# One matmul with 32 copies of each bias column in place of four with 128

## The reference, cut to what matters

```python
bias_h = rel_bias.astype(jnp.float32).T            # (4 heads, 32 buckets)
...
dist_own = qp[:, None] - (qblk * BLK + offs)[None, :]
s_own = (jnp.einsum('bhqd,bhkd->bhqk', qc, kown)
         + bias_h[:, t5_bucket(jnp.maximum(dist_own, 0))][None])
s_own = jnp.where(dist_own >= 0, s_own, NEG_INF)
```

## Time and profile before

| what | us |
| --- | --- |
| median of 3 runs | 1577.85 (1576.73 to 1578.09) |
| the profiled execution's own time | 1576.61 |
| its span, first to last instruction | 1574.8 |
| PE busy | 1333.2 (85%) |
| DVE busy | 423.2 (27%) |
| ACT busy | 278.7 (18%) |
| POOL busy | 180.0 (11%) |
| DMA, mean over the span | 316 GB/s |

### The profile page before, as it was taken

How to read it: one execution, slowest core, us unless ns; L and a number is a source line. 1 busy time by engine, 2 the same in 40 slices (tenths; PEclk the granted TensorE clock), 3 DMA queues, 4 the chain that set the end, 5 groups by cost and what they waited for, 6 DMA issues and landing times. The chain is left out here.

```text
span 1574.8 us, 22184 instructions
## 1 busy us (share of the span) xinstructions
PE 1333.2 (85%) x9378; PEld 719.3 (46%) x9378; DVE 423.2 (27%) x842; ACT 278.7 (18%) x544; POOL 180.0 (11%) x122
## 2 busy tenths in 40 slices
PE   9999999999999999776776767899999676676776
PEld 4855456545879564322322323655554232232332
DVE  3443343523565531120000100257321010010011
ACT  2132310323412121210000000105211111011010
POOL 0450033300000005692000000000000000000000
PEclk9999999999999999898898999999999989899789
DMA  9923442254640499999999999944799999999997
GB/s 383 346 81 140 180 160 107 80 187 161 231 160 31 165 387 405 429 427 429 429 427 429 428 427 429 387 183 165 285 406 426 427 427 427 428 427 426 429 427 323
DMA packets 44867, 498.20 MB, mean 316 GB/s; under 512 B 6656, under 2 KB 8960, under 8 KB 12544
## 3 DMA queue, kind: packets, MB, share of 16 engines
q1 hardware_dynamic: 44800, 497.22, 77.0%
HBM read 495.11 MB, written 2.10 MB: 316 GB/s over the span
## 5 line engine op out<-in xcount | busy, mean ns | idle before, releaser
L2858 PE MATMUL banks<-weight_ring,arena 128*32 128x512 f32 x1472 | 212.9, 710 | 126.1 <-DMA weight_ring<-in_moe_weights 126.0
L2776 DVE TENSOR_TENSOR arena<-arena,banks 64x512 f32<-64x512 f32 x32 | 22.1, 690 | 656.2 <-ACT arena L2713 656.2
L2858 PEld LDWEIGHTS banks<-weight_ring,arena 128*32 128x32 f32 x1472 | 45.2, 120 | 277.7 <-DMA weight_ring<-in_moe_weights 139.3
L2833 PE MATMUL banks<-arena,x 128*128 128x64 f32 x960 | 115.2, 280 | 0.0
L2833 PEld LDWEIGHTS banks<-arena,x 128*128 128x128 f32 x960 | 114.8, 199 | 0.0
L323 PE MATMUL banks<-weight_ring,hT 128*128 128x512 f32 x256 | 112.3, 593 | 0.0
L2869 PE MATMUL banks<-weight_ring,arena 128*32 128x512 f32 x728 | 89.3, 617 | 21.6 <-DMA weight_ring<-in_moe_weights 9.6
L2713 ACT ACTIVATE arena<-banks 64x512 f32<-64x512 f32 x32 | 18.9, 590 | 490.0 <-PE banks L2858 490.0
L2903 PE MATMUL banks<-arena 64*128 64x512 f32 x240 | 59.6, 615 | 21.0 <-ACT arena L2719 21.0
L323 PEld LDWEIGHTS banks<-weight_ring,hT 128*128 128x128 f32 x256 | 48.1, 190 | 57.2 <-issue 56.9
L2858 PE MATMUL banks<-arena 128*32 128x512 f32 x352 | 56.9, 668 | 14.0 <-DMA arena<-in_moe_weights 14.0
(11 more groups left out here) (529 smaller groups left out, 1756.5 us busy)
## 6 DMA issues: line engine op xcount, KB each, us to landing
weight_ring<-in_moe_weights SPq DMA_DIRECT2D x137, 2048.0 KB, 26.8
weight_ring<-in_ring_weights SPq DMA_DIRECT2D x35, 2048.0 KB, 9.0
arena<-in_moe_weights SPq DMA_DIRECT2D x18, 2048.0 KB, 43.9
spare_weights<-in_moe_weights SPq DMA_DIRECT2D x10, 2048.0 KB, 43.9
mix<-in_moe_weights SPq DMA_DIRECT2D x9, 2048.0 KB, 47.5
arena<-in_moe_weights SPq DMA_DIRECT2D x17, 1024.0 KB, 42.1
x_normed<-in_moe_weights SPq DMA_DIRECT2D x9, 1024.0 KB, 39.1
hT<-in_moe_weights SPq DMA_DIRECT2D x9, 1024.0 KB, 46.3
```

The source lines that it names most:

```text
L2776: dve.tensor_tensor(hid[0:2 * CAP, :], sil[0:2 * CAP, :], b_gu[2 * CAP:4 * CAP, :], ALU.mult).then_inc(s_h, 1)
L2833: ins = pe.matmul((b_x, b_dn)[k // 4][:, k % 4 * 2 * CAP:(k % 4 + 1) * 2 * CAP], g.x[:, tt, k * P:(k + 1) * P], Pr[:, tt, :], start=(tt == ...
L2858: ins = pe.matmul(b_gu[q:q + CAP, :], xg[:, 2 * quarter + k, e * CAP:(e + 1) * CAP], up_w(where, quarter, e)[:, which, k, :], start=(quart ...
```

## The change

One product takes the place of four: its 128 columns of weights are 32 copies of each head's column, so rows 32h to 32h+31 of the result are head h's. `tables` is spread to 4x32 columns in place of 4x128, `rows` is 128x511 in place of 4 such tiles, and ACT makes one copy. Each of the four DMAs to DRAM still writes 128x511 values, but reads 32 partitions, each four times. The waits are counted accordingly (one product, one copy), and the wait for the scaled tables ahead of the fourth product goes.

```diff
--- before.py
+++ after.py
@@ -457,9 +457,9 @@
     pb = sT
     pbT = [rqk_flat[:, h * 3 * P:(h + 1) * 3 * P] for h in range(RH)]
     rqk = rqk_flat.rearrange("p (h t) -> p h t", h=8)
-    tables = rqk_flat[:, 0:4 * P].rearrange("p (h m) -> p h m", h=4)
+    tables = rqk_flat[:, 0:P].rearrange("p (h m) -> p h m", h=4)
     rv, mv = (v_flat[:, i * 1024:(i + 1) * 1024].rearrange("p (a n) -> p a n", a=TT) for i in range(2))
-    rows = v_flat[:, 0:4 * 511].rearrange("p (h j) -> p h j", h=4)
+    rows = v_flat[:, 0:511]
     scratch = nc.dram_tensor("bias_rows", (4, P, 511), F32).ap()
     sm = g.small
     x_first = g.mix[:, 0:KT + KT * S]
@@ -544,8 +544,9 @@
             sp.dma_start(gcol[1], A["norm_g"][1]).then_inc(s_gain[1], 16)
             sp.dma_start(gcol[2], A["even_norm_g"]).then_inc(s_gain[2], 16)
             for h in range(4):
-                sp.wait_ge(s_rc, h + 1)
-                sp.dma_start(scratch[h], rows[:, h, :]).then_inc(s_w, 16)
+                sp.wait_ge(s_rc, 1)
+                sp.dma_start(scratch[h].rearrange("(r c) j -> r c j", c=4),
+                             rows[32 * h:32 * h + 32, :].unsqueeze(1).to_broadcast([32, 4, 511])).then_inc(s_w, 16)
             for l in range(DEPTH):
                 sp.dma_start(rgain[l], A["ret_norm_g"][l].partition_broadcast(P)).then_inc(s_wide[l], 16)
                 sp.dma_start(pgain[l], A["ple_norm_g"][l].partition_broadcast(P)).then_inc(s_wide[l], 16)
@@ -642,9 +643,8 @@
                 copy_out(q, 3)
                 qk_root(q, 1)
                 if l == 0:
-                    for h in range(4):
-                        act.wait_ge(s_r, h + 1)
-                        act.copy(rows[:, h, :], ps[h][:, 0:511]).then_inc(s_rc, 1)
+                    act.wait_ge(s_r, 1)
+                    act.copy(rows, ps[0][:, 0:511]).then_inc(s_rc, 1)
                 for b in range(4):
                     act.wait_ge(*q.qkt(b + 1))
                     c = 2 if b < 2 else 1
@@ -788,13 +788,13 @@
                         TT_(scaled[i], con[name], ps[3][:, 0:S], ALU.mult).then_inc(s_tb, 1)
                     dve.wait_ge(s_tb, 2)
                     dve.wait_ge(s_tab, 16)
-                    dve.tensor_copy(tables, table.unsqueeze(2).to_broadcast([P, 4, P])).then_inc(s_t, 1)
+                    dve.tensor_copy(tables, table.unsqueeze(2).to_broadcast([P, 4, 32])).then_inc(s_t, 1)
                 qk_normed(q, 0)
                 dve.wait_ge(s_qkg[l], 32)
                 link(dve, dve.tensor_scalar(qkg[l][:, 2:3], qkg[l][:, 0:1], P ** -0.5, None, ALU.mult))
                 qk_normed(q, 1)
                 if l == 0:
-                    dve.wait_ge(s_r, 4)
+                    dve.wait_ge(s_r, 1)
                 for b in range(4):
                     rotated(q, l, b)
                 for h in range(RH):
@@ -999,16 +999,14 @@
                 if l == 0:
                     pe.wait_ge(s_c, 16)
                     pe.wait_ge(s_t, 1)
-                    for h in range(4):
-                        if h == 3:
-                            pe.wait_ge(s_tb, 2)
-                        pe.matmul(ps[h][:, 0:511], tables[0:64, h, :], con["buckets"][0:64, :], start=True, stop=True).then_inc(s_r, 1)
+                    pe.matmul(ps[0][:, 0:511], tables[0:64].rearrange("p h m -> p (h m)"), con["buckets"][0:64, :],
+                              start=True, stop=True).then_inc(s_r, 1)
                 for u in (4, 5):
                     pe.wait_ge(*q.ev(u - 3))
                     project(l, u)
                 pe.wait_ge(*q.qkn(TT))
                 if l == 0:
-                    pe.wait_ge(s_rc, 4)
+                    pe.wait_ge(s_rc, 1)
                 for b in range(4):
                     for hh in range(2):
                         for tt in range(TT):
```

## The result

| kernel | median us | lowest to highest | runs | ratio to before [95% interval] |
| --- | --- | --- | --- | --- |
| before | 1577.85 | 1576.63 to 1578.12 | 9 | |
| changed | 1581.69 | 1579.31 to 1584.25 | 9 | 1.0028 [1.0019, 1.0037] |

The change makes the kernel slower by 0.28%, 3.8 us; the forecast was 2.6 us faster. The profiled execution took 1581.25 us, with a span of 1579.5, 4.7 longer than before. The nine runs of the changed kernel spread over 4.9 us, those of before over 1.5; in a later set of 23 runs those of before spread over 3.9, so the change is not shown to widen it.

What follows compares the result with a forecast made beforehand. PE was taken to bound the early layers, the expert-weight DMA stream the experts, its start following PE. PE -2.6 us, 0 for the rest: 1577.85 - 2.6 = 1575.2 us; range from 1.4 below 1575.2 up to 1577.3.

Steps and rivals of the forecast that it cites:

- six records of 0.43 us: PE's bias products near 36 us: six of eight records go, 2.58 us saved, taken as 2.6.
- P1: PE product that ACT copies later; expected at 65.9 us in place of 68.50.
- DVE, ACT and SP give and cost nothing: Smaller spreading copy, three fewer ACT copies and the rewritten DMAs near 25 to 55 us: 0 for the sum.
- The adds at L733: DVE adds held beside POOL; the one due at 61.4 us might end at 64.8, costing 0 with 1.1 us left.
- the fourfold bound: Upper bound on the bias writes' landing: four times 10.3 us, or 31 us more, if one partition's reads queue up.
- the half rate that was weighed: Skill's port rule for 32-partition transfers: each bias write's landing up to twice as long, at most 10 us, sum unchanged.
- that wait moves with PE: The one 1.6 us PE wait from 35 to 200 us, before the retention outputs (L1037), needs values from PE product P4.
- PE time saved at 36 us should arrive at the end nearly whole: Conclusion that PE's early lead also shifts the expert-weight stream's start; the whole 2.6 us arrives, chance 0.80.
- the three rivals: Saving swallowed wholly or half (1577.8 or 1576.5 us, 0.13); repeated-read write lands late (1586, 0.03); larger saving (1574.7, 0.04).
- The rival for slower: Repeated-read write lands late, DVE waits for the bias before U2: 31 us later, 11 arrive, 1586 us; chance 0.03.
- slower by over 0.2%: Outcome class beyond the 3.2 us a measurement can tell: late landing plus a little for runs apart, chance 0.04.
- The signs listed for a wrong forecast: PE's lead shrunk by 600 us (something fixed in time holds it), or there at 600 and gone at 1000.

Runs made afterwards that it cites:

- e4: Kernel before with its four products and copies, but each of the four transfers to DRAM reads 32 partitions four times; 1577.65 us, ratio 1.0000.
- e6: Changed kernel with eleven in place of eight warming matmuls at the start, where TensorE waits for its first weights; 1574.30 us, ratio 0.9978.
- e1: Changed kernel with three one-column matmuls put ahead of the one product, restoring TensorE's instruction count; 1575.66 us, ratio 0.9988.
- f1: Changed kernel with the 2 MB expert-weight load issued at 1024 us held until the row at L2260 is done; 1576.48 us, ratio 0.9989.
- e7: Kernel before with six of the 128 products in the row at L2262 each waited for before the next starts; 1587.18 us, ratio 1.0062.
- e5: Changed kernel run once more from the same source, for a second profile; 1582.65 us, ratio 1.0031.
- e2: Kernel before with five in place of eight warming matmuls at the very start; 1585.71 us, ratio 1.0046.

## Why the prediction was wrong

- Right: six records of 0.43 us go; 2.57 us against 2.6. The transposes came at 50.15 (50.3 forecast), P1 at 65.71 (65.9).
- Right: DVE, ACT and SP give and cost nothing. The adds at L733 were held at 45.68 and 52.59 (3.82 and 1.86 us), the one at 61.24 was not (0.71 us); scores were not delayed.
- Right: the repeated reads are free (e4). The landing was not slower at all, so neither the fourfold bound nor the half rate that was weighed shows in this transfer; the price of an issue, 0.75 to 0.84 us for 0.33 to 0.43, had been missed and was covered. That the landing is the same beside other traffic does not test the half rate of a transfer that runs alone.
- Right, with the positions kept: a lead of PE at 36 us reaches the end nearly whole. e6 is 3.1 us below its runs of before (1577.44), e1 2.3; in e6's profile the lead is 2.58 us at 60 us and 2.4 at the end.
- **Wrong:** the step from "that wait moves with PE" to "PE time saved at 36 us should arrive at the end nearly whole". It took the rest of PE's stream as given, and so put the fetch of its instructions at nothing. The view of waits went to 200 us only, but a longer one would not have shown it: the waits of before list what held PE up before, and they cannot list a fetch that was in time. Removing twelve instructions moved 16 KB boundaries by twelve places in all code behind, and at L2260 a margin of about 2.8 us (from a packet at -0.6 to the 2.2 that the row bears) was gone. Price in the first profile: 1 us at L1602, and 5.2 at L2260, of which 1.4 is the gap and most of the rest the halved clock behind it. The other 1.1 of the 7.4 us from a lead of 2.8 to a lag of 4.6 are the low clock at 557 us (0.7) and the first experts.
- None of the three rivals was this one. The rival for slower had the right sign with the wrong mechanism, and all of "slower by over 0.2%" had a chance of 0.04.
- The signs listed for a wrong forecast did work: the lead was 2.79 at 440 us and about 0.5 at 632. But they named "something fixed in time" as the cause, which it was not.

What stays open: why a fetch is issued late enough to meet the load (f1 shows the load matters, not how the packet is queued); what brings the low clock at 557, 1134 to 1142 and 1179 us in some executions (it costs 0.7 us at 557); and what e7's longer runs add.

## What to carry to other kernels

A long unrolled program has one more resource that no edit names: the place of its instructions in the fetched blocks. Where a row of very short matmuls runs beside a full DMA, an edit far ahead that changes the number of TensorE's instructions can open or close a gap there, which here was worth twice the edit itself. So look in the profile after for "issue" waits inside rows that were whole, and try a few pads where the engine waits anyway before judging an edit of a few microseconds.

## What the runs showed of the hardware

- In a row of 256 records of 29 ns (L2260), TensorE idled 1.4 to 2.6 us behind record 150 in all three profiles with the layout of the changed kernel and the load beside it (changed, e5, e2); the instruction packet started 3.65 to 4.75 us into the row. It did not idle where the packet started by 1.4 us.
- In a row of 192 records of 16 ns (L1602) it idled 0.1 to 0.75 us with a packet that started 0.15 to 0.65 us into the row, and not at all with one that started ahead of it. The record at which the row breaks moved by two (148, 146, 144) with each matmul (two records, each with a weight load) at the start of the program.
- Gaps of 1.4, 1.7 and 2.6 us in the row at L2260 were followed within 0.3 to 2.1 us by granted clock 0.50 for 6.8, 10.3 and 6.9 us; the same row without a gap or pauses kept 1.00.
- A DMA that reads each of 32 partitions four times landed as soon as one that reads 128 once, and cost SP twice the issue time.
